# Retention and FFN of a hybrid decoder block: two state buffers, two results per PSUM bank, and another chunk order in the FFN

## The chip, the cores and the metric

The kernel runs on all 8 cores of one Trainium2 chip. Each core does one half (1024 own positions) of one of four sequences; cores exchange nothing. The metric is the device time in microseconds of the slowest core. An engine here is one of TensorE (PE, matmuls; PEld is its weight load), VectorE (DVE), ScalarE (ACT), GpSimd (POOL, which here only issues the weight loads) and SyncE (SP, which issues the other DMAs).

## What is computed

The block runs MoBA attention and RetNet retention side by side, merges them by sigmoid gates, and ends in a gated MLP with a causal depthwise convolution of width 3. Cut to the two parts that matter here:

```python
# retention, per head, chunks of 128 positions
scores = einsum('bhnid,bhnjd->bhnij', qc, kc) * inner_decay
inner  = einsum('bhnij,bhnje->bhnie', scores, vc)
kv     = einsum('bhnjd,bhnje->nbhde', kc * k_decay, vc)
def step(state, kv_n):                     # state is (128, 256) per head
    return chunk_decay * state + kv_n, state
_, prev = scan(step, 0, kv)
cross  = einsum('bhnid,nbhde->bhnie', qc * q_decay, prev)
yr     = head_group_norm(inner + cross, g) * silu(gr)
# FFN
u = causal_depthwise_conv(h2 @ w_up, conv_w, conv_b)
val, gt = split(u, 2)
x = x + gate2 * ((silu(gt) * val) @ w_down)
```

## The kernel before

The program lists its operations in one order in Python. A small scheduler (`Sched`) puts each into the queue of its engine, in that order, and makes it wait, by semaphores, for the last writer and the readers of what it touches. Each engine works its queue strictly in order. What counts as the same memory is coarse: blocks of 512 bytes in SBUF, and a whole bank in PSUM (`keys`, which returns one key for every tile whose name begins with `ps`). Two results in different halves of one bank are therefore one thing to the scheduler. `bank()` hands out the eight PSUM banks in rotation; weights come as slabs of 256 columns through `slab_load`, with four slab buffers in rotation, issued on POOL. `mm` is line 378, `tp` 382, `act` 399, `ts` 408 (one scalar) or 410 (two), `tt` 413, `stt` 419, `recip` 422, `acopy` 428, `vcopy` 431.

**Retention** (four groups `rg` of two heads `m`, eight heads in all). A group projects q and k with rotary. Then each head does, in this order:

1. `proj_tm` projects vr: 16 tiles of 128 positions, two to a bank, 256 matmuls of 256 columns, each bank evacuated by one VectorE cast.
2. The kv part: for n = 0 to 14 one matmul of `kdT` chunk n with `vr` chunk n into 256 columns of a bank of its own. VectorE copies the first into the state `Sst`, and updates the state in place with each further one (`stt`: state times decay plus product). At n = 7 ScalarE copies the state to `Sbh`; at n = 8 VectorE multiplies it by `flag` (`ts`); from n = 8 on ScalarE copies it to `Sb[n-8]` before VectorE may overwrite it; after the last update it is copied to `Sb[7]`.
3. Scores: eight matmuls of 128 columns, four to a bank; VectorE multiplies them by the decay into `sT`, and q by its decay into `qdT` (8 and 8 products).
4. The gate projection, 8 tiles, 128 matmuls of 256 columns in four banks. Each bank is copied by VectorE into `sgtmp` and put through a silu on ScalarE. A halo of two positions follows (16 matmuls, `psh`), copied into `ynh`.
5. Eight group norms c = 0 to 7: two matmuls (`sT`, `qdT`) into 256 columns of a bank of its own, then `groupnorm_gate`: bn_stats and bn_aggr on VectorE, a square root on ScalarE, and on VectorE the reciprocal, an affine that reads the bank (`ts`, L410), and two products. A small ninth for the halo, with `ynh` as its scratch tile, ends the head.

**FFN up part** (22 pairs `fp`). A pair has two slabs of `w_up`: `slv` for the value, `slg` for the gate. `up_chunk` does one chunk: two banks of 16 matmuls of 512 columns, a halo of 16 matmuls of 2 columns, and then on VectorE `conv`: two `ts` over 512 columns, four wide `stt` and four of one or two columns. For each of m = 0, 1 come value chunk, gate chunk, the silu of `ug` on ScalarE into `sgt`, and the product with `uv` on VectorE into `actT`. The buffers `uv`, `ug` and `sgt` alternate with the pair's m. At eight values of fp (1, 4, 7, 10, 13, 16, 19, 21) `mod_row_slab` comes first, 16 matmuls that read `s_rep2`. `s_rep2` lies right behind `sgt[1]` and shares its last 512-byte block.

Of the kernel before, what the change touches and what calls it, by code (L numbers as in the profile page):

```python
# [8 lines left out]
F32 = mybir.dt.float32  # L9
BF16 = mybir.dt.bfloat16  # L10
ALU = mybir.AluOpType
AF = mybir.ActivationFunctionType
# [256 lines left out]
def build_program(stop_after=None, debug=()):  # L269
# [10 lines left out]
    cd = _const_tables(1)["chunk_decay"]  # L280
    X1KEYS = [("x1s", d) for d in range(8)]

    with contextlib.ExitStack() as st:
# [38 lines left out]
        AA = Arena(A_t, 98304)  # L322
# [19 lines left out]
        flag = CA.alloc(F32, [128, 1])  # L342
# [34 lines left out]
        def mm(out, lhsT, rhs, start, stop):  # L377
            S.op("pe", lambda e: e.matmul(out, lhsT, rhs, start=start, stop=stop),  # L378
                 reads=[lhsT, rhs], writes=[out])
# [21 lines left out]
        def ts(out, in0, s1, s2, op0, op1=None):  # L401
            r = [in0]
            if not isinstance(s1, float):
                r.append(s1)
            if s2 is not None and not isinstance(s2, float):
                r.append(s2)
            if op1 is None:
                S.op("dve", lambda e: e.tensor_scalar(out, in0, s1, None, op0), reads=r, writes=[out])
            else:
                S.op("dve", lambda e: e.tensor_scalar(out, in0, s1, s2, op0, op1), reads=r, writes=[out])  # L410

        def tt(out, in0, in1, op):
            S.op("dve", lambda e: e.tensor_tensor(out, in0, in1, op), reads=[in0, in1], writes=[out])  # L413

        def stt(out, in0, sc, in1, op0, op1):
            r = [in0, in1]
            if not isinstance(sc, float):
                r.append(sc)
            S.op("dve", lambda e: e.scalar_tensor_tensor(out, in0, sc, in1, op0, op1), reads=r, writes=[out])  # L419
# [7 lines left out]
        def acopy(out, in_):  # L427
            S.op("act", lambda e: e.copy(out, in_), reads=[in_], writes=[out])

        def vcopy(out, in_):  # L430
            S.op("dve", lambda e: e.tensor_copy(out, in_), reads=[in_], writes=[out])  # L431
# [11 lines left out]
        def bank():  # L443
            b = bank_ctr[0] % 8
            bank_ctr[0] += 1
            return psb[b][:]
# [319 lines left out]
        Sb = AA.alloc(BF16, [128, 8, 256])  # L766
# [8 lines left out]
        Sbh = AA.alloc(BF16, [128, 256])  # L775
        zth = AA.alloc(BF16, [128, 512])
        ynh = AA.alloc(F32, [128, 256])
# [1 line left out]
        rgb = AA.alloc(F32, [128, 512])  # L779
        decTh = AA.alloc(F32, [128, 128])  # L780
        qdech = AA.alloc(F32, [128, 128])
        Sst = AA.alloc(F32, [128, 256])
        r32a = [AA.alloc(F32, [128, 512]) for _ in range(2)]
        r32b = [AA.alloc(F32, [128, 512]) for _ in range(2)]
        yn = [AA.alloc(F32, [128, 256]) for _ in range(2)]
# [22 lines left out]
        for rg in range(4):  # L808
# [20 lines left out]
            for m in range(2):  # L829
                h = 2 * rg + m  # L830
# [8 lines left out]
            for m in range(2):  # L839
                h = 2 * rg + m  # L840
# [2 lines left out]
                slv = slab_load(din["w_in"], 0, NKC, 5120 + h * 256)  # L843
                proj_tm(slv, list(range(16)), lambda i: vr[:, i:i + 2, :])
                for n in range(15):
                    o = bank()[:, 0:256]
                    mm(o, kdT[:, m, n, :], vr[:, n, :], True, True)
                    if n == 0:
                        vcopy(Sst, o)
                    else:  # L850
                        if n == 7:
                            acopy(Sbh, Sst)
                        if n == 8:
                            ts(Sst, Sst, flag[:, 0:1], None, ALU.mult)
                        if n >= 8:
                            acopy(Sb[:, n - 8, :], Sst)
                        stt(Sst, Sst, cd[h], o, ALU.mult, ALU.add)
                acopy(Sb[:, 7, :], Sst)
                for c4 in range(2):
                    pss = bank()  # L860
                    for u in range(4):
# [16 lines left out]
                vcopy(ynh[0:2, :], psh[0:2, 0:256])  # L878
                act(sgh[0:2, :], ynh[0:2, :], AF.Silu)
                for c in range(8):  # L880
                    o = bank()[:, 0:256]
                    mm(o, sT[:, c, :], vr[:, 8 + c, :], True, False)
                    mm(o, qdT[:, c, :], Sb[:, c, :], False, True)
                    groupnorm_gate(o, 128, c % 2, rgb[:, m * 256:(m + 1) * 256], sg[:, c, :], yn[c % 2],
                                   zt[:, c, m * 256:(m + 1) * 256])
# [174 lines left out]
        def up_chunk(sl, m, ch, dst, hi):  # L1060
            ps2 = [proj_fm(sl, m, lambda kc, th=th: h2T[:, kc, th * 512:(th + 1) * 512]) for th in range(2)]
            psh = proj_fm(sl, m, lambda kc: h2Th[:, kc, :], w=2)
            ts(Phs[:, hi, :], psh[:, 0:2], flag[:, 0:1], None, ALU.mult)
            conv(dst, ps2, Phs[:, hi, :], ch)

        fctr = [0]
        for fp in range(22):
            g2sched = {1: 0, 4: 1, 7: 2, 10: 3, 13: 4, 16: 5, 19: 6, 21: 7}
            if fp in g2sched:
                mod_row_slab(5, g2bc, s_rep2, g2sched[fp])  # L1070
            slv = slab_load(din["w_up"], 0, NKC, fp * 256)
            slg = slab_load(din["w_up"], 0, NKC, FFN + fp * 256)
            for m in range(2):
                fc = fp * 2 + m
                i = fctr[0] % 2
                fctr[0] += 1
                up_chunk(slv, m, fc, uv[i], 0)
                up_chunk(slg, m, 44 + fc, ug[i], 1)
                act(sgt[i], ug[i], AF.Silu)
                tt(actT[:, fc, :], uv[i], sgt[i], ALU.mult)  # L1080
        dump("actT", actT, [128, NFC, 1024], BF16)
        if stop_after == "H":
            return finish()
# [52 lines left out]
```

How the kernel before makes its waits and increments, by code:

```python
                def body(engobj):  # L117
                    waited = {}
                    for rec in ops[e]:
                        need = {}
                        for (de, di) in rec["deps"]:
                            drec = ops[de][di]
                            s = ("d", drec["dma"]) if drec["dma"] is not None else ("e", de)
                            need[s] = max(need.get(s, 0), drec["cnt"])
                        for s, v in need.items():
                            if waited.get(s, 0) >= v:
                                continue
                            waited[s] = v
                            sem = dsem[s[1]] if s[0] == "d" else esem[s[1]]
                            engobj.wait_ge(sem, v)
                        ins = rec["fn"](engobj)
                        if rec["dma"] is not None:
                            ins.then_inc(dsem[rec["dma"]], 16)
                        elif rec["signal"]:
                            ins.then_inc(esem[e], 1)
                    if e == "sp":
                        for k in final_wait:
                            engobj.wait_ge(dsem[k], 16 * self.dma_cnt[k])
```

## Time and profile before

| | us |
|---|---|
| median of 2 runs | 4114.99 (4110.7 and 4119.28) |
| profiled execution, device time | 4106.44 |
| its span on core 3, the slowest | 4104.8 (the cores: 4080.4 to 4104.8) |
| TensorE busy | 3050.6 (74%) |
| VectorE busy | 2048.4 (50%) |
| ScalarE busy | 496.5 (12%) |
| mean granted clock of TensorE, all cores | 0.843 to 0.846 |

All rows shown in this document are of the slowest core. In a timeline row the first number is the start in us from the span's beginning, the second how long the row lasts (x4 means four instructions merged), and the bracket gives the engine's idle time just before it with what ended it. A granted clock of 1.00 is 2.4 GHz on TensorE and 0.50 is 1.2 GHz. Matmul ends are modelled, so starts are surer than ends.

### The profile page before, as it was taken

The numbers are of one execution on the slowest core, as the hardware profiler recorded it, in microseconds if no ns is written. First come the engines' busy times: TensorE is split into PE (matmuls) and PEld (weight loads), VectorE is DVE, ScalarE is ACT, GpSimd is POOL, SyncE is SP. The second block draws the span as 40 slices with busy tenths as digits, with TensorE's granted clock in tenths as the row PEclk, the third lists the DMA queues.
The fourth block names the chain that finished last, engine by engine and source line by source line (L and its number), as shares of the span: only waits on it lengthen the run. The fifth ranks groups of instructions, "written<-read, shape, count | busy, mean of one in ns | idle before, by whom it ended". The sixth has DMA issues, their size and how long they took to land.

```text
span 4104.8 us, 57818 instructions; the slowest of 8 cores (4080.4 to 4104.8 us)
## 1 busy us (share of the span) xinstructions
PE 3050.6 (74%) x21160; PEld 1826.4 (44%) x21160; DVE 2048.4 (50%) x4111; ACT 496.5 (12%) x1016; POOL 218.3 (5%) x198
## 2 busy tenths in 40 slices
PE   0137767878678876766775999986368888888999
PEld 0122522325323553534554444455334444444888
DVE  0287555576555546455455322222377777776111
ACT  0021023311223010111111111100110000000000
POOL 1100000000000000000000010011000000000000
PEclk9998955589555888887887999987679999999999
DMA  9932200012000223123231866799935555555785
GB/s 117 152 118 31 27 5 1 3 34 32 11 1 1 51 28 66 23 57 42 44 53 17 130 83 84 90 158 179 176 64 73 72 72 73 72 72 80 119 139 96
DMA packets 435370, 282.02 MB, mean 69 GB/s; under 512 B 6794, under 2 KB 422794, under 8 KB 431506
## 3 DMA queue, kind: packets, MB, share of 16 engines
q0 software_dynamic: 384176, 195.10, 38.2%
q1 hardware_dynamic: 50916, 83.22, 6.8%
q8 instruction: 174, 2.85, 0.3%
q14 instruction: 104, 0.85, 0.1%
HBM read 452.41 MB, written 20.97 MB: 115 GB/s over the span
## 4 chain that ended last, share of the span: by engine, by line
PE 52%; DVE 27%; DMA 9%; issue 7%; ACT 4%; DVEq 1%; ACTq 0%; SPq 0%; POOL 0%; POOLq 0%
PE ps L378 50%; DVE hT L419 6%; DVE A L422 5%; DMA slab<-w_ada 5%; DVE hT L410 5%; DVE A L413 2%; ACT A L399 2%; DVE A L419 2%; DMA slab<-w_o 2%; PE ps L382 2%; DVE A L410 1%; DVE A L431 1%; ACT hT L399 1%; DVEq L130 1%; DVE C L799 1%
## 5 line engine op out<-in xcount | busy, mean ns | idle before, releaser
L378 PE MATMUL ps<-hT,slab 128*128 128x512 bf16 (+1 forms) x6144 | 1343.2, 377 | 2.8 <-DVE A L431 1.8
L378 PEld LDWEIGHTS ps<-hT,slab 128*128 128x128 bf16 x6144 | 584.6, 99 | 696.3 <-issue 56.5
L378 PE MATMUL ps<-slab,hT 128*128 128x256 bf16 (+1 forms) x4352 | 518.9, 285 | 101.5 <-ACT hT L399 93.0
L378 PE MATMUL ps<-A 128*128 128x256 bf16 (+3 forms) x1560 | 475.1, 363 | 115.7 <-ACT A L399 83.5
L378 PEld LDWEIGHTS ps<-slab,hT 128*128 128x128 bf16 (+1 forms) x4352 | 440.1, 102 | 177.8 <-issue 108.4
L399 ACT ACTIVATE A<-A 128x256 bf16<-128x256 f32 (+6 forms) x744 | 341.8, 470 | 1282.3 <-DVE A L431 596.9
L378 PE MATMUL ps<-slab,A 128*128 128x256 bf16 x3968 | 452.3, 278 | 46.5 <-DMA slab<-w_o 34.3
L378 PEld LDWEIGHTS ps<-slab,A 128*128 128x128 bf16 x3968 | 395.0, 100 | 99.9 <-issue 46.9
L378 PEld LDWEIGHTS ps<-A 128*128 128x128 bf16 (+1 forms) x1560 | 173.3, 113 | 411.5 <-issue 384.0
L419 DVE SCALAR_TENSOR_TENSOR hT<-ps,hT 128x511 f32<-128x511 f32 (+1 forms) x528 | 301.9, 572 | 56.1 <-DVE hT L419 1.4
L378 PE MATMUL ps<-A,C 128*128 128x256 bf16 (+3 forms) x552 | 210.3, 384 | 118.6 <-ACT A L399 98.1
L410 DVE TENSOR_SCALAR A<-ps,C 128x256 f32<-128x256 f32 (+2 forms) x432 | 196.6, 467 | 169.5 <-PE ps L378 93.2
L413 DVE TENSOR_TENSOR A<-ps,A 128x512 f32<-128x512 f32 (+5 forms) x360 | 181.3, 511 | 180.9 <-PE ps L378 123.3
L378 PE MATMUL ps<-C,slab 128*128 128x2 bf16 x3328 | 106.7, 164 | 206.2 <-DMA slab<-w_ada 131.2
L431 DVE COPY A<-ps 128x512 f32<-128x512 f32 (+2 forms) x216 | 117.5, 551 | 264.6 <-PE ps L378 217.2
L431 DVE CAST A<-ps 128x512 bf16<-128x512 f32 (+1 forms) x144 | 96.7, 686 | 265.3 <-PE ps L378 237.4
L378 PEld LDWEIGHTS ps<-C,slab 128*128 128x128 bf16 x3328 | 105.0, 97 | 237.9 <-issue 209.5
L413 DVE TENSOR_TENSOR ps<-ps,A 128x256 f32<-128x256 f32 x136 | 58.5, 430 | 271.7 <-PE ps L378 268.2
L422 DVE RECIPROCAL A<-A 128x512 f32<-128x512 f32 (+1 forms) x56 | 162.2, 2897 | 49.3 <-ACT A L399 49.3
L399 ACT ACTIVATE hT<-hT 128x1024 f32<-128x1024 f32 (+1 forms) x52 | 61.8, 1188 | 1015.3 <-DVE hT L419 646.7
L369 POOL DMA_DIRECT2D slab<-w_in x52 | 60.2, 1159 | 2095.4 <-PE ps L378 1506.4
L378 PE MATMUL ps<-C,A 128*128 128x2 bf16 (+1 forms) x136 | 12.8, 168 | 201.0 <-DVE C L800 174.7
(69 smaller groups left out, 1557.8 us busy)
## 6 DMA issues: line engine op xcount, KB each, us to landing
slab<-w_in POOLq DMA_DIRECT2D x52, 1024.0 KB, 9.2
slab<-w_ada POOLq DMA_DIRECT2D x48, 1024.0 KB, 22.5
slab<-w_up POOLq DMA_DIRECT2D x44, 1024.0 KB, 9.5
A<-xw SPq DMA_DIRECT2D x24, 1024.0 KB, 7.2
hT<-x1s SPq DMA_DIRECT2D x16, 1024.0 KB, 8.1
slab<-w_down POOLq DMA_DIRECT2D x16, 1024.0 KB, 9.7
slab<-w_ret_br POOLq DMA_DIRECT2D x8, 1024.0 KB, 10.6
slab<-w_o POOLq DMA_DIRECT2D x8, 1024.0 KB, 33.9
```

Of the source, the lines that this page charges most:

```text
L130: engobj.wait_ge(sem, v)
L369: S.op("pool", lambda e: e.dma_start(out=out, in_=in_), reads=reads, writes=writes, dma=key)
L378: S.op("pe", lambda e: e.matmul(out, lhsT, rhs, start=start, stop=stop), reads=[lhsT, rhs], writes=[out])
L382: S.op("pe", lambda e: e.matmul(out, in_, ident, start=True, stop=True), reads=[in_, ident], writes=[out])
L399: S.op("act", lambda e: e.activation(out, in_, func, **kw), reads=r, writes=w)
L410: S.op("dve", lambda e: e.tensor_scalar(out, in0, s1, s2, op0, op1), reads=r, writes=[out])
L413: S.op("dve", lambda e: e.tensor_tensor(out, in0, in1, op), reads=[in0, in1], writes=[out])
L419: S.op("dve", lambda e: e.scalar_tensor_tensor(out, in0, sc, in1, op0, op1), reads=r, writes=[out])
L422: S.op("dve", lambda e: e.reciprocal(out, in_), reads=[in_], writes=[out])
L431: S.op("dve", lambda e: e.tensor_copy(out, in_), reads=[in_], writes=[out])
L799: S.op("dve", lambda e: e.bn_stats(bnst[0:np_, bi, :], o), reads=[o], writes=[bnst[0:np_, bi, :]])
```

## The change

Four edits, in three places of the program.

```diff
-        Sst = AA.alloc(F32, [128, 256])
+        Sst2 = [AA.alloc(F32, [128, 256]), ynh]
...
                 for n in range(15):
-                    o = bank()[:, 0:256]
+                    if n % 2 == 0:
+                        pskv = bank()
+                    o = pskv[:, (n % 2) * 256:(n % 2) * 256 + 256]
                     mm(o, kdT[:, m, n, :], vr[:, n, :], True, True)
+                    cur, nxt = Sst2[n % 2], Sst2[(n + 1) % 2]
                     if n == 0:
-                        vcopy(Sst, o)
+                        vcopy(nxt, o)
                     else:
                         if n == 7:
-                            acopy(Sbh, Sst)
+                            acopy(Sbh, cur)
                         if n == 8:
-                            ts(Sst, Sst, flag[:, 0:1], None, ALU.mult)
+                            ts(cur, cur, flag[:, 0:1], None, ALU.mult)
                         if n >= 8:
-                            acopy(Sb[:, n - 8, :], Sst)
-                        stt(Sst, Sst, cd[h], o, ALU.mult, ALU.add)
-                acopy(Sb[:, 7, :], Sst)
+                            acopy(Sb[:, n - 8, :], cur)
+                        stt(nxt, cur, cd[h], o, ALU.mult, ALU.add)
+                acopy(Sb[:, 7, :], Sst2[1])
...
                 for c in range(8):
-                    o = bank()[:, 0:256]
+                    if c % 2 == 0:
+                        psy = bank()
+                    o = psy[:, (c % 2) * 256:(c % 2) * 256 + 256]
...
             for m in range(2):
+                up_chunk(slv, m, fp * 2 + m, uv[m], 0)
+            for m in range(2):
                 fc = fp * 2 + m
-                i = fctr[0] % 2
-                fctr[0] += 1
-                up_chunk(slv, m, fc, uv[i], 0)
-                up_chunk(slg, m, 44 + fc, ug[i], 1)
-                act(sgt[i], ug[i], AF.Silu)
-                tt(actT[:, fc, :], uv[i], sgt[i], ALU.mult)
+                up_chunk(slg, m, 44 + fc, ug[m], 1)
+                act(sgt[m], ug[m], AF.Silu)
+                tt(actT[:, fc, :], uv[m], sgt[m], ALU.mult)
```

The state alternates between a buffer of its own and the halo's scratch tile `ynh`: each update reads one and writes the other. Two kv products, and two group norms, share a bank, left half and right half. The FFN does both value chunks of a pair before its gate chunks. The number and kinds of instructions on every engine stay the same.

TensorE in the kv part of the first head, its end: products n = 11 to 14 (128x256 into a bank `psN`, `A<-` the arena that holds kdT and vr), the scores (128x128), and the first tile of the gate projection (from slab and hT; d_15 is its slab's DMA). Before:

```order
L378 MATMUL ps3<-A 128x256 [waits s_dve]
L378 MATMUL ps4<-A 128x256 [waits s_dve]
L378 MATMUL ps5<-A 128x256 [waits s_dve]
L378 MATMUL ps6<-A 128x256 [waits s_dve]
L378 MATMUL ps7<-A 128x128 [waits s_dve]
L378 MATMUL ps7<-A 128x128 x3
L378 MATMUL ps0<-A 128x128 [waits s_dve]
L378 MATMUL ps0<-A 128x128 x3
L378 MATMUL ps1<-slab,hT 128x256 [waits s_dve,d_15]
L378 MATMUL ps1<-slab,hT 128x256 x31
```

After the change the same place, from n = 10:

```order
L378 MATMUL ps5<-A 128x256
L378 MATMUL ps5<-A 128x256 [waits s_dve]
L378 MATMUL ps6<-A 128x256
L378 MATMUL ps6<-A 128x256 [waits s_dve]
L378 MATMUL ps7<-A 128x256
L378 MATMUL ps0<-A 128x128 x4
L378 MATMUL ps1<-A 128x128 x4
L378 MATMUL ps2<-slab,hT 128x256 [waits d_15]
L378 MATMUL ps2<-slab,hT 128x256 x31
```

Every product before waits for VectorE (s_dve) in a bank eight allocations old; after it, the left half (first of two rows with one bank) waits for nothing, the right half waits for VectorE to have read the left one, and scores and gate projection have no wait for VectorE.

TensorE in the group norms of the same head, two matmuls to a norm (the first of `sT`, the second of `qdT`), c = 1 to 3, before:

```order
L378 MATMUL ps7<-A 128x256
L378 MATMUL ps7<-A 128x256 [waits s_act]
L378 MATMUL ps0<-A 128x256
L378 MATMUL ps0<-A 128x256 [waits s_dve,s_act]
L378 MATMUL ps1<-A 128x256 [waits s_dve]
L378 MATMUL ps1<-A 128x256 [waits s_act]
```

After the change, the same three norms:

```order
L378 MATMUL ps7<-A 128x256 [waits s_dve]
L378 MATMUL ps7<-A 128x256 [waits s_act]
L378 MATMUL ps0<-A 128x256
L378 MATMUL ps0<-A 128x256 [waits s_act]
L378 MATMUL ps0<-A 128x256 [waits s_dve]
L378 MATMUL ps0<-A 128x256 [waits s_act]
```

c = 1 and c = 3 now share a bank with the norm ahead of them, and their first matmul waits for VectorE.

VectorE in the second pair of the FFN, where the second chunk's conv ends (banks 2, 3) and the third's begins (halo in ps7, banks 5, 6), before, where the second chunk is the gate chunk of m = 0:

```order
L419 SCALAR_TENSOR_TENSOR hT<-ps2,hT 128x1
L419 SCALAR_TENSOR_TENSOR hT<-ps2,hT 128x2
L419 SCALAR_TENSOR_TENSOR hT<-C,hT 128x1
L419 SCALAR_TENSOR_TENSOR hT<-C,hT 128x2
L413 TENSOR_TENSOR A<-hT 128x1024
L408 TENSOR_SCALAR C<-ps7,C 128x2
L410 TENSOR_SCALAR hT<-ps5,hT 128x512
L410 TENSOR_SCALAR hT<-ps6,hT 128x512
```

After the change, where the second chunk is the value chunk of m = 1 and the third is the gate chunk of m = 0:

```order
L419 SCALAR_TENSOR_TENSOR hT<-ps2,hT 128x1
L419 SCALAR_TENSOR_TENSOR hT<-ps2,hT 128x2
L419 SCALAR_TENSOR_TENSOR hT<-C,hT 128x1
L419 SCALAR_TENSOR_TENSOR hT<-C,hT 128x2
L408 TENSOR_SCALAR C<-ps7,C 128x2
L410 TENSOR_SCALAR hT<-ps5,hT 128x512
L410 TENSOR_SCALAR hT<-ps6,hT 128x512
```

The product (L413, 128x1024) is gone from between them; it now stands behind the third chunk, and the other behind the fourth as before.

## Rows read from the trace of the kernel before

**Rows 1.** windows: retention, FFN up part; stretch, busy per engine (instructions), PEclk, DMA, GB/s
```profile
1374.00:2310.00 936.00, 657.50 (x4906) 468.58 (x4903) 484.31 (x1119) 100.69 (x213) 31.42 (x28) 0.84 0.30 49
...
3014.00:3789.00 775.00, 675.65 (x4358) 331.01 (x4356) 548.38 (x1048) 46.72 (x44) 59.23 (x52) 0.93 0.55 70
```

**Rows 2.** timeline of one kv part; start, us, engine, line, operation [idle before <-releaser]
```profile
1659.13 0.41 DVE L431 COPY A<-ps 128x256 f32<-128x256 f32 x1
...
1659.65 0.42 DVE L419 SCALAR_TENSOR_TENSOR A<-A,ps 128x256 f32<-128x256 f32 x1
...
1660.22 0.27 PE L378 MATMUL ps<-A 128*128 128x256 bf16 x1 [0.26 <-DVE A L419]
...
1660.84 2.00 DVE L419 SCALAR_TENSOR_TENSOR A<-A,ps 128x256 f32<-128x256 f32 x4 [0.17 <-DVE A L419]
...
1664.09 0.35 DVE L408 TENSOR_SCALAR A<-A,C 128x256 f32<-128x256 f32 x1
...
1666.98 17.81 PE L378 MATMUL ps<-slab,hT 128*128 128x256 bf16 x144 [0.67 <-DVE A L419]
...
1672.25 0.42 DVE L419 SCALAR_TENSOR_TENSOR A<-A,ps 128x256 f32<-128x256 f32 x1 [0.72 <-ACT A L428]
1672.59 2.46 DVE L413 TENSOR_TENSOR A<-ps,A 128x128 bf16<-128x128 f32 x8
```

**Rows 3.** timeline, first and last of the eight heads: kv's first evacuation, gate projection
```profile
1431.46 0.41 DVE L431 COPY A<-ps 128x256 f32<-128x256 f32 x1
...
1439.17 17.39 PE L378 MATMUL ps<-slab,hT 128*128 128x256 bf16 x144 [0.57 <-DVE A L419]
...
2199.95 0.41 DVE L431 COPY A<-ps 128x256 f32<-128x256 f32 x1
...
2207.56 17.19 PE L378 MATMUL ps<-slab,hT 128*128 128x256 bf16 x144 [0.57 <-DVE A L419]
```

**Rows 4.** timeline of another head's kv part: one product at half clock
```profile
1746.21 0.37 PE L378 MATMUL ps<-A 128*128 128x256 bf16 x1 [0.26 <-DVE A L419]
1746.73 0.42 DVE L419 SCALAR_TENSOR_TENSOR A<-A,ps 128x256 f32<-128x256 f32 x1 [0.66 <-PE ps L378]
```

**Rows 5.** timeline of VectorE, group norms of one head: eight full ones, then the halo's
```profile
1691.33 0.54 DVE L410 TENSOR_SCALAR A<-ps,C 128x256 f32<-128x256 f32 x1
...
1692.85 0.42 DVE L799 BATCH_NORM_STATS2 C<-ps 128x6 f32<-128x256 f32 x1
...
1712.04 0.42 DVE L799 BATCH_NORM_STATS2 C<-ps 2x6 f32<-2x256 f32 x1 [0.84 <-PE ps L378]
```

**Rows 6.** waits (total us, times, longest) and lines by form, retention stage
```profile
DVE A L419 <- ACT A L428: 40.1, 57, 1.0
...
L431 DVE COPY A<-ps 2x256 f32<-2x256 f32 x8 | 3.3, 411 | 3.3 <-PE ps L378 3.3
```

**Rows 7.** windows around gate and vr projection; the column after POOL is the granted clock
```profile
1663.50:1666.90 3.40, 1.17 (x8) 0.70 (x8) 1.62 (x4) 0.84 (x3) 0.00 (x0) 0.57 1.39 187
1666.90:1670.00 3.10, 3.02 (x15) 2.19 (x16) 0.88 (x3) 1.18 (x3) 0.00 (x0) 0.50 0.05 7
...
1671.00:1672.00 1.00, 1.00 (x12) 0.89 (x10) 0.42 (x1) 0.33 (x1) 0.00 (x0) 1.00 0.00 0
...
1720.00:1741.00 21.00, 21.00 (x195) 18.81 (x194) 4.15 (x6) 0.00 (x0) 0.00 (x0) 1.00 0.00 1
```

**Rows 8.** timeline of VectorE after a drain in the FFN; last row from the waits
```profile
3172.17 0.22 DVE L408 TENSOR_SCALAR C<-ps,C 128x2 f32<-128x2 f32 x1 [8.15 <-PE ps L378]
...
3179.48 0.22 DVE L408 TENSOR_SCALAR C<-ps,C 128x2 f32<-128x2 f32 x1 [0.59 <-PE ps L378]
...
3187.15 1.22 DVE L413 TENSOR_TENSOR A<-hT 128x1024 bf16<-128x1024 f32 x1 [1.31 <-ACT hT L399]
...
3202.62 1.23 DVE L413 TENSOR_TENSOR A<-hT 128x1024 bf16<-128x1024 f32 x1 [1.36 <-ACT hT L399]
...
PE ps L378 <- ACT hT L399: 93.0, 8, 12.1
```

## The prediction

> **What bounds the kernel now.** I read the spans and clocks first: the profiled run is 4106.4 us, 8.6 us under the median 4115.0, so my sum is made against 4106.4 and 8.6 is added at the end. Then the stretches by stage [rows 1]. The change touches two: retention (936 us, TensorE busy 657) and the FFN's up part (775 us, TensorE busy 676, VectorE 548).
>
> Retention, for each of its 8 heads, is a chain of turns. TensorE projects vr (256 matmuls), computes 15 kv products and the scores, projects the gate (128 matmuls), then waits for eight group norms. The timeline of one kv part [rows 2] shows how it runs now: each product has a bank of its own, so TensorE is up to eight products ahead and only waits for VectorE to free the bank of eight allocations ago (the matmul at 1660.22). VectorE takes a state update in 0.42 us, started every 0.53 us ((2.00-0.42)/3). For the later updates it hands over to ScalarE, which copies the single state away, before it may overwrite it: 40.1 us of VectorE waits over the stage [rows 6]. TensorE does not care: it starts the gate projection at 1666.98, when update 9 frees a bank, while VectorE works on until 1672.67 (1672.25+0.42). From kv's first evacuation (1659.13) to the gate projection is 7.85 us here, 7.71 in the first head and 7.61 in the last of the eight [rows 3].
>
> Who decides the end of the gate projection? VectorE sits idle for TensorE before the copy that ends it (the halo's, 2x256): 3.3 us over 8 heads, 0.4 each [rows 6]. So TensorE's start time passes to the end with nearly no slack, and the 40.1 us of handovers lie beside TensorE's projection.
>
> In the FFN, TensorE gives a chunk (two 512-column products and a halo) every 7.31 us (VectorE's starts at 3172.17 and 3179.48 both wait for it [rows 8]). VectorE needs 6.4 to 6.7 us for its conv (3172.17 to 3179.48-0.59; 3179.48 to 3187.15-1.31), plus per pair of chunks a wait of 1.31 us for the silu and a product of 1.22. So VectorE is the slower of the two, 15.5 us a pair (3187.15 to 3202.62) against 14.6, except just after a drain. Eight times, 93.0 us in all, TensorE waits [rows 8] for the last silu, because s_rep2 begins in the 512-byte block that ends sgt[1].
>
> **The change part by part.**
>
> *kv, packed.* Dependencies go by whole bank, so product n (odd) must wait until VectorE has read product n-1. A step then has a length that alternates. Odd: VectorE's end to the matmul's start 0.15 (update 1 ends at 1659.65+0.42=1660.07, the matmul starts at 1660.22 [rows 2]), the matmul 0.27 at full clock or 0.37 at half clock [rows 2, 4], 0.10 to 0.15 to VectorE (1746.58 to 1746.73 [rows 4]), the update 0.42: 0.94 to 0.99 warm, 1.04 to 1.09 cold. Even: the matmul follows its twin at once, so the update comes 0.52 to 0.59 after the last one ends. Step 8 has the flag multiplication too: 0.35 [rows 2] plus an update and two gaps of 0.10, 0.97, up to 1.05.
>
> TensorE gets past product 13 only after update 12. From the end of the first evacuation that is six odd steps (three warm at 0.97, three cold at 1.07: 6.1), five even at 0.55 (2.75), step 8 (1.0): 9.9 us. Then 0.15, products 13 and 14, and eight score matmuls of 128 columns. At full clock 195 matmuls of 256 columns take 21.0 us, 0.108 each [rows 7]; the half clock adds 0.10 (0.37 against 0.27), so 0.21, and half of that for 128 columns. The granted clock is 0.57 from 1663.5 to 1666.9 and 0.50 after it [rows 7], so I take cold: 2x0.21+8x0.105=1.26. Gate projection at 9.9+0.15+1.26=11.3 us after the evacuation's end; now it is 7.85-0.41=7.4. **Later by 3.9 us a head.** Where VectorE, not TensorE, came last before (the 0.4 is a mean), a tenth or two are lost: 3.75x8 = **+30 us**. Bounds: all warm and shortest, 6x0.94+5x0.52+0.97+0.15+0.65=10.0, +2.6 a head, +21; all cold and longest, 6x1.09+5x0.59+1.05+0.15+1.26=12.0, +4.6, +37.
>
> *Two state buffers.* They take ScalarE's copies out of the chain: update n writes the other buffer, whose copy began two updates before. VectorE would have finished update 14 at 9.9+1.07+0.55=11.5 us instead of 13.1 (1672.67-1659.54 [rows 2]). Those 1.6 us are worth nothing: what comes next for VectorE (16 products, 2.46 us for 8 [rows 2], so until 16.4) is done before TensorE's second gate pair at 11.3+2x32x0.108=18.2, and each further one comes 3.5 us later. ynh as the second buffer adds only orders on VectorE that are met anyway.
>
> *Group norm, packed.* Product c (odd) now waits until VectorE's affine of c-1 has read the bank. Between that affine's end (1691.33+0.54) and the next bn_stats (1692.85) lie 0.98 us in which VectorE does its other two products [rows 5]. The round trip VectorE, two cold 256-column matmuls, VectorE is on record: 0.84 us idle at 1712.04 [rows 5]. It fits with 0.14 to spare: cost 0. Without that cover it would be 0.84 x 4 x 8 = 27 us; a shortfall of 0.1 gives 3.
>
> A rule speaks against packing. By these rows TensorE runs eight banks ahead in kv, and loses that lead. The Trainium skill, Perfetto Trace Analysis, section Matmul Optimizations, says "Ensure all 8 PSUM banks are being leveraged to maximize available instruction-level parallelism"; for kv the trace agrees (my 11.3 us against 7.4). Taken literally for the group norms too, the rule would charge the 27 us that the 0.98 us gap hides.
>
> *FFN order.* v0 g0 v1 g1 becomes v0 v1 g0 g1. TensorE's work and its rate stay. VectorE still has each product right behind its own silu, so the wait of 1.31 us [rows 8] stays, at all 44 products. What differs is the start after a drain. Now: v0, wait 0.59, g0, silu wait and product (1.31+1.22), by which time v1 has been there for a while. After: v0, wait 0.59, v1, then another wait for TensorE (3179.48+7.31=3186.79, a conv that starts at 3179.48 is done at 3185.84: 0.95). **0.9 us** later, not made good, since VectorE has no idle time until the next drain. Nine such stretches (the start and eight drains): **+8 us**; 0 to 8.5. slv's slots come free 7.3 us earlier, but no wait for a weight slab exists here to be shortened. The last chunk before each drain is g1 in both, so the 93.0 us stay.
>
> *Queues.* DMAs are neither added nor moved among themselves. 88 fewer banks are drawn over 8 heads, a multiple of 8, so later stages meet the same bank numbers.
>
> **Sum:** 4106.4+30+8 = 4144.4 in the profile's terms, with 8.6 beside the median **4153 us**, 0.9% slower.
>
> **The rivals.**
>
> *A, VectorE decides (not slower).* If the end of a head followed VectorE's chain and not TensorE's, the handovers removed would count: 1.6 us a head, 13 us less, and with +8 in the FFN 4101 (4110 beside the median). It decides if TensorE's gate projection has over 3.9 us of slack. Against it: VectorE is seen idle for TensorE right there [rows 6]. Chance 0.08.
>
> *B, the clock stays low (clearly slower).* TensorE idles longer in kv. Today the granted clock is 0.50 for the first 3 us of the gate projection and recovers by 1671 [rows 7]. If it stayed low through all 128 matmuls, the some 100 that now run at full clock cost 0.10 more each: 10 us a head, 80 in all: 4233, as much as 2%. Against: after the group norms TensorE has idled for 22 us and more, and by 1720, 9 us into the next projection, it has the full clock [rows 7]. A 4 us longer gap is mild. By the Trainium skill, TensorE: Matmul & The Clock Gate, section What's actually happening, idleness halves the clock and sustained work releases it; the trace agrees with its 0.50 and 1.00. Chance 0.03.
>
> *C, the group norms are exposed.* If the second matmul's result reached VectorE as late as if nothing hid it, +27 us: 4180 beside the median. For it: only 0.14 us is spare. Against: a small shortfall costs a tenth, not the whole. Chance 0.06.
>
> *Forecast as above.* 0.83.
>
> **How the numbers follow.** Lowest of the forecast: 4106.4+21+0=4127, highest 4106.4+37+8.5+3=4155; with 8.6, and 5 us for scatter (the two runs read 4110.7 and 4119.3), the likeliest case alone is 4131 to 4169. The range 4122 to 4174 takes in part of C's 4180 and leaves out A and B. A measurement here tells about 2% (82 us) from no change. Over 2% slower: B, and a little for what I have not seen, 0.04. Over 2% faster needs 82 us where the whole kv parts last 8x13: 0.01. Within 2%: 0.95.
>
> **What would show it.** In kv: update pairs every 1.5 to 1.65 us, alternating short and long gaps, TensorE's wait for VectorE in half the products, no wait of VectorE for ScalarE, and the first evacuation to the gate projection at 11 to 12 us; the copy 2x256 with a VectorE wait of several us. Group norms still 2.97 us apart. FFN: about 104 us between drains instead of 103. I am wrong if the first evacuation to the gate projection stays under 10 us, if that shift does not reach the head's end, or if the group norms' pace changes.

## The result, and the profile after

| | before | after |
|---|---|---|
| median of all runs, us | 4118.1 | 4211.7 |
| fastest run, us | 4101.0 | 4148.0 |
| ratio after to before | | 1.0123, 95% interval 1.0066 to 1.0181 |
| profiled execution, us | 4106.4 | 4163.9 |
| spans of the eight cores, us | 4080.4 to 4104.8 | 4120.2 to 4162.4 |

The changed kernel is 1.2% slower. The median of all its runs is no measure, since in about half of them the cores of one die had a lower clock and the time was up to 4476 us; the ratio leaves such runs of both kernels out. The forecast was 4153 us; 4118.1x1.0123 is 4169. The profiled execution lies some 14 us above the fastest ones: from the last head to the FFN, where the change touches nothing, its slowest core took 790 us, another core of the same execution 771, and the profiled core of before 762. On the slowest cores of the two kernels and of nine of the ten experiments (all but the first with the FFN order alone), this unchanged stretch takes 762 to 790 us, so a difference of under 28 us between two single device times says little. So I compare stretches, not whole spans. Rows of after are of its core 7, the slowest.

The first fence answers [rows 1]: windows of retention and of the FFN's up part after the change (same columns; the second is moved to where the FFN now lies).

```profile
1374.00:2310.00 936.00, 647.85 (x4732) 456.08 (x4730) 469.64 (x1092) 100.59 (x211) 28.26 (x25) 0.81 0.28 46
3065.00:3840.00 775.00, 677.64 (x4368) 331.58 (x4365) 541.46 (x1039) 46.57 (x44) 58.09 (x51) 0.93 0.54 70
```

By the first row, retention holds fewer matmuls in the same 936 us (4732 against 4906) at a lower granted clock (0.81 against 0.84). The FFN's shares are nearly those of before.

The next fence is the timeline of the first head's kv part after the change, and answers [rows 2] and [rows 4].

```profile
1422.99 0.41 DVE L431 COPY A<-ps 128x256 f32<-128x256 f32 x1
...
1423.55 0.38 PE L378 MATMUL ps<-A 128*128 128x256 bf16 x2 [1.17 <-DVE A L431]
1423.92 0.42 DVE L419 SCALAR_TENSOR_TENSOR A<-A,ps 128x256 f32<-128x256 f32 x1 [0.52 <-PE ps L378]
1424.52 0.42 DVE L419 SCALAR_TENSOR_TENSOR A<-A,ps 128x256 f32<-128x256 f32 x1 [0.17 <-DVE A L419]
...
1425.09 0.38 PE L378 MATMUL ps<-A 128*128 128x256 bf16 x2 [1.16 <-DVE A L419]
...
1430.33 0.58 PE L378 MATMUL ps<-A 128*128 128x256 bf16 x2 [1.51 <-DVE A L419]
1430.95 0.42 DVE L419 SCALAR_TENSOR_TENSOR A<-A,ps 128x256 f32<-128x256 f32 x1 [0.76 <-PE ps L378]
...
1435.12 17.37 PE L378 MATMUL ps<-slab,hT 128*128 128x256 bf16 x144
```

The matmul rows come as pairs now (x2: the right half of one bank and the left half of the next), each started 0.15 us after an update's end: 1424.52+0.42=1424.94, matmuls at 1425.09. The updates come in twos. The gate projection (x144) starts at 1435.12, 12.13 us after the first evacuation; in the last head it is 12.02:

```profile
2219.51 0.41 DVE L431 COPY A<-ps 128x256 f32<-128x256 f32 x1
...
2231.53 8.66 PE L378 MATMUL ps<-slab,hT 128*128 128x256 bf16 x70
```

Over the eight heads the mean of this distance is 12.24 us (11.85 to 12.66) against 7.76 before. It is nearly the whole of the story in retention: 4.5 of the 4.8 us by which a head grows. The next rows are the group norms of the first head and answer [rows 5]:

```profile
1455.68 0.54 DVE L410 TENSOR_SCALAR A<-ps,C 128x256 f32<-128x256 f32 x1
...
1456.37 1.01 PE L378 MATMUL ps<-A 128*128 128x256 bf16 x4 [3.55 <-DVE A L410]
...
1457.27 0.42 DVE L799 BATCH_NORM_STATS2 C<-ps 128x6 f32<-128x256 f32 x1
...
1461.73 0.55 DVE L410 TENSOR_SCALAR A<-ps,C 128x256 f32<-128x256 f32 x1
...
1462.42 1.01 PE L378 MATMUL ps<-A 128*128 128x256 bf16 x4 [5.05 <-DVE A L410]
1463.26 0.42 DVE L799 BATCH_NORM_STATS2 C<-ps 128x6 f32<-128x256 f32 x1
```

Norm 1's matmuls (x4 with norm 2's) start 0.15 us after the affine's end (1456.22), and bn_stats comes at 1457.27, 1.05 us after that end; norm 3's comes at 1463.26, 0.98 after 1462.28. Both are as before the change, where norm 1 of the first head had the same 1.05 us (1459.74+0.54 to 1461.33) with a bank of its own:

```profile
1459.74 0.54 DVE L410 TENSOR_SCALAR A<-ps,C 128x256 f32<-128x256 f32 x1
...
1461.33 0.42 DVE L799 BATCH_NORM_STATS2 C<-ps 128x6 f32<-128x256 f32 x1
```

Waits over the stage (total us, times, longest) and a line by form, both after the change, answer [rows 6]:

```profile
PE ps L378 <- DVE A L410: 149.5, 32, 5.4
...
DVE A L419 <- ACT A L428: 7.3, 11, 0.7
```

```profile
L431 DVE COPY A<-ps 2x256 f32<-2x256 f32 x8 | 3.3, 412 | 8.5 <-PE ps L378 8.5
```

TensorE waits 149.5 us for the affines, in 32 places, and VectorE's pace in the norms does not change. VectorE's waits for ScalarE's state copies fell from 40.1 us to 7.3. The forecast was none, and the rows behind the 7.3 need not be real waits: update 11 of the first head starts at 1432.73, just after a copy that ended at 1432.58, but the copy that it depends on by the program had ended at 1431.86. VectorE's wait before the halo's copy rose from 3.3 to 8.5 us, 1.0 to 1.15 us in every head: TensorE is now plainly the last to come. The clock answers [rows 7]:

```profile
1427.00:1435.00 8.00, 2.87 (x16) 1.43 (x16) 4.19 (x11) 2.96 (x8) 0.00 (x0) 0.55 0.66 90
1435.00:1438.00 3.00, 3.00 (x18) 2.14 (x16) 2.54 (x10) 0.69 (x2) 0.00 (x0) 0.51 0.03 8
1438.00:1440.00 2.00, 2.00 (x20) 1.80 (x19) 1.62 (x7) 0.00 (x0) 0.00 (x0) 1.00 0.00 0
```

After the gate projection's start the clock stays at half for nearly three microseconds more. The FFN answers [rows 8], the timeline of VectorE after a drain, then a row of the waits:

```profile
3120.29 0.22 DVE L408 TENSOR_SCALAR C<-ps,C 128x2 f32<-128x2 f32 x1 [8.12 <-PE ps L378]
...
3127.70 0.22 DVE L408 TENSOR_SCALAR C<-ps,C 128x2 f32<-128x2 f32 x1 [1.03 <-PE ps L378]
...
3134.91 0.22 DVE L408 TENSOR_SCALAR C<-ps,C 128x2 f32<-128x2 f32 x1 [0.49 <-PE ps L378]
...
3142.58 1.23 DVE L413 TENSOR_TENSOR A<-hT 128x1024 bf16<-128x1024 f32 x1 [1.31 <-ACT hT L399]
```

```profile
PE ps L378 <- ACT hT L399: 97.1, 8, 13.1
```

VectorE waits 1.03 us for TensorE before the second chunk and 0.49 before the third. The wait before the third is new; the two together are 1.52 us, where the forecast had 0.59 and 0.95. The product of m = 0 begins at 3142.58, 22.29 us after the start of the first conv, with three convs ahead of it; it was 14.98 before, with two.

### The profile page after: what moved, and what is told of

Its sections match the earlier page's. It is cut to its first block, busy times and chain, and to the rows that moved or that the text cites. A ratio compares the mean times of both kernels' runs of the same rounds, so it can differ in the third digit from the quotient of the medians.

```text
span 4162.4 us, 57672 instructions; the slowest of 8 cores (4120.2 to 4162.4 us)
## 1 busy us (share of the span) xinstructions
PE 3067.4 (74%) x21160; PEld 1826.8 (44%) x21160; DVE 2048.8 (49%) x4111; ACT 497.1 (12%) x1016; POOL 218.2 (5%) x198
## 4 chain that ended last, share of the span: by engine, by line
PE 58%; DVE 23%; DMA 9%; issue 6%; ACT 3%; DVEq 1%; ACTq 0%; SPq 0%; POOL 0%; POOLq 0%
PE ps L378 56%; DVE A L422 5%; DVE hT L410 4%; DMA slab<-w_ada 3%; DVE hT L419 3%; DVE A L413 2%; DVE A L419 2%; DMA A<-xw 2%; ACT A L399 2%; PE ps L382 2%; DVE A L410 1%; DVE A L431 1%; DMA slab<-w_o 1%; DVEq L130 1%; DVE C L799 1%
## 5 line engine op out<-in xcount | busy, mean ns | idle before, releaser
L378 PE MATMUL ps<-A 128*128 128x256 bf16 (+3 forms) x1560 | 492.6, 377 | 305.9 <-DVE A L410 149.5
L413 DVE TENSOR_TENSOR A<-ps,A 128x512 f32<-128x512 f32 (+5 forms) x360 | 181.3, 511 | 172.3 <-PE ps L378 117.3
L413 DVE TENSOR_TENSOR ps<-ps,A 128x256 f32<-128x256 f32 x136 | 58.5, 430 | 293.7 <-PE ps L378 290.2
L413 DVE TENSOR_TENSOR A<-A 128x512 bf16<-128x512 f32 (+5 forms) x289 | 135.2, 475 | 33.3 <-DMA A<-b_g 5.6
```

## The experiments

In the numbers below, "gate" is the mean distance over eight heads from kv's first evacuation to the start of the gate projection, "head" the mean from that evacuation to the halo's bn_stats, and "FFN" the stretch from the first 512-column matmul to the first down matmul. "Device" is the time of the profiled execution in us, or, as a number near 1, the ratio to the kernel before, which was run beside each.

| kernel | gate | head | FFN | device |
|---|---|---|---|---|
| before | 7.76 | 52.2 | 775.0 | 4106, medians 4118 to 4122 |
| after | 12.24 | 57.0 | 781.5 | 1.0123 |
| kv unpacked | 6.43 | 51.6 | 781.1 | 0.9993 |
| buffers only | 6.44 | 51.7 | 774.7 | 4105 |
| norms only | 7.75 | 52.1 | 776.4 | 4103 |
| FFN order only | 7.9 | 52.6 | 783.3 | 4119 |
| kv packed only | 13.82 | 58.7 | 779.1 | 4160 |
| kv in pairs | 3.37 | 48.0 | 781.1 | 4115 |
| FFN aligned | 7.9 | 52.9 | 664.0 | 4006 |
| after, FFN aligned | 12.28 | 57.0 | 666.0 | 4050 |
| all that helped | 3.45 | 47.9 | 665.1 | 0.9624 |

**One edit undone: kv unpacked.** The kernel after, with

```diff
-                    if n % 2 == 0:
-                        pskv = bank()
-                    o = pskv[:, (n % 2) * 256:(n % 2) * 256 + 256]
+                    o = bank()[:, 0:256]
                     mm(o, kdT[:, m, n, :], vr[:, n, :], True, True)
```

> The changed kernel with one edit undone: each kv product has a bank of its own again; the two state buffers, the packed group norms and the new FFN order stay. My theory: the loss sits in TensorE's wait inside the kv part. The gate projection then starts when update 9 frees its bank, and with two buffers update 9 ends at about 7 x 0.55 + 1.0 + 0.55 = 5.4 us after the first evacuation's end, so first evacuation to gate projection is about 6.1 us (7.8 before, 12.2 changed). The head (first evacuation to the halo's bn_stats) is about 50.6 us (52.2 before, 57.0 changed), the FFN stretch stays at 782. Device time about 6 us under the kernel before. Rival (the buffers or the packed norms cost, not the kv packing): first evacuation to gate projection stays near 12, device time stays 40 to 50 us above the kernel before.

Gate 6.43 us (expected 6.1), head 51.6 us, FFN 781.1 us, ratio 0.9993 (0.9979 to 1.0008). The whole loss of the change goes with this edit (what is left of it, 6 us more in the FFN and 5 us less in the eight heads, cancels). In the timeline of its first head (VectorE, then TensorE):

```profile
1424.11 0.41 DVE L431 COPY A<-ps 128x256 f32<-128x256 f32 x1
...
1425.29 0.42 DVE L419 SCALAR_TENSOR_TENSOR A<-A,ps 128x256 f32<-128x256 f32 x1 [0.17 <-DVE A L419]
...
1425.89 0.42 DVE L419 SCALAR_TENSOR_TENSOR A<-A,ps 128x256 f32<-128x256 f32 x1 [0.17 <-DVE A L419]
...
1430.40 17.84 PE L378 MATMUL ps<-slab,hT 128*128 128x256 bf16 x144
```

the updates follow each other every 0.59 us with no alternation, and the gate projection starts 6.29 us after the evacuation. The head is 51.6, not the 50.6 I expected: the next experiment says why.

**The two buffers alone.** The kernel before with `Sst2`, `cur` and `nxt` as in the diff of the change, and nothing else.

> The kernel before with the two state buffers alone. Theory that TensorE's place in the order decides: VectorE's chain to update 9 is shorter by the handovers, so the gate projection starts 1.6 us earlier (6.1 us after the first evacuation against 7.8), the head takes 50.6 us against 52.2, 13 us less over eight heads. Theory that VectorE's chain decides: update 14 ends 4 to 5 us earlier and the head gets shorter by that, 48 us, 35 us less in all. Theory that the buffers are worth nothing because the copies lie beside TensorE's projection: 52.2.

Gate 6.44 us (expected 6.1), 1.3 us earlier than before; head 51.7 us, so only 0.5 us of it arrived (4 us over eight heads), and the stretch from the gate projection's start to the first bn_stats is 18.57 us where it was 17.80. VectorE's chain does not decide, or the gain would be 4 us a head. Windows after the start of the gate projection show where it went. The second head with the buffers alone (its gate projection starts at 1514.77):

```profile
1514.80:1518.00 3.20, 3.20 (x16) 2.21 (x17) 2.20 (x6) 2.03 (x6) 0.00 (x0) 0.50 0.63 85
1518.00:1520.00 2.00, 2.00 (x15) 1.52 (x14) 1.67 (x7) 0.27 (x1) 0.00 (x0) 0.70 0.00 0
```

The second head of the kernel before (start 1521.73):

```profile
1521.70:1524.00 2.30, 2.27 (x11) 1.61 (x12) 0.84 (x2) 0.90 (x3) 0.00 (x0) 0.50 0.03 4
1524.00:1526.00 2.00, 2.00 (x21) 1.76 (x19) 0.84 (x2) 0.64 (x2) 0.00 (x0) 1.00 0.00 0
```

With the buffers the clock is at half for 3.2 us and at 0.70 in the 2 us after; before it is at half for 2.3 us and at full speed in the next 2. The start of the dense work came earlier and the clock did not come with it.

The same can be counted in every head, with windows of 0.25 us over the first 7 us of the gate projection. The time at half clock in them is 2.8 us before (2.2 to 3.8), 4.4 us with the buffers alone (3.7 to 5.3) and 4.2 us with kv unpacked (3.8 to 5.2). In all 72 heads of the nine kernels without pairs, the stretch from the gate projection's start to the first bn_stats is 16.3 to 16.4 us plus half of that time. So the 1.6 us more at half clock are the missing 0.8 us, and TensorE decides when the norms start in every one of these heads.

How large this is depends on what it is held against. Four kernels have the kv part of before (before, norms only, FFN order only, FFN aligned), with heads of 52.2, 52.1, 52.6 and 52.9 us; in 5 of their 32 heads TensorE was at half clock for 5.2 to 5.9 us, in the other 27 for 2.2 to 3.8. Against their mean, 52.5 us, the two kernels with a gate of 6.4 gain 0.85 us a head out of 1.4.

**The packed group norms alone.** The kernel before with `psy` as in the diff.

> The kernel before with the packed group norms alone. My theory: the round trip of 0.84 us hides in the 0.98 us of the two products, so the norms stay 2.97 us apart and the stretch from the first bn_stats to the halo's stays at 26.6 us. Rival (exposed): four norms of eight start up to 0.8 us later, 29 to 30 us for the stretch, up to 27 us in all.

From the first bn_stats to the halo's, 26.6 us in the mean as before; head 52.1 us. VectorE's affines and bn_stats of the first head, from the affine of norm 0 on:

```profile
1443.38 0.55 DVE L410 TENSOR_SCALAR A<-ps,C 128x256 f32<-128x256 f32 x1
...
1444.96 0.42 DVE L799 BATCH_NORM_STATS2 C<-ps 128x6 f32<-128x256 f32 x1
...
1449.42 0.54 DVE L410 TENSOR_SCALAR A<-ps,C 128x256 f32<-128x256 f32 x1
...
1450.94 0.42 DVE L799 BATCH_NORM_STATS2 C<-ps 128x6 f32<-128x256 f32 x1
```

Norm 1 comes 1.03 us after the affine's end (1443.93 to 1444.96) and norm 3 0.98 after (1449.96 to 1450.94), as in the kernel before (1.05 and 0.98): hidden, as forecast, and these rows show no cost.

**The FFN order alone**, in two experiments with the same kernel.

> The kernel before with the new FFN order alone. My theory: VectorE waits for TensorE once more after each of the nine restarts, so the FFN stretch (first 512-column matmul to the first down matmul) is 782 us against 775, and retention heads stay at 52.2 us. Rival (the order changes nothing and the 7 us come from elsewhere): 775.

> The kernel before with the new FFN order alone, timed in rounds. My theory: 7 us more in the FFN stretch (782 against 775), heads at 52.2 us, so device time 4122 to 4125, a ratio of 1.001 to 1.003, which the interval may not clear. Rival (more than half of the 1.2% loss comes from the FFN): ratio 1.006 or more.

FFN 781.7 us in the first (read on core 7, whose span was 4104.9 us; the three device times were 4376 to 4426) and 783.3 us in the second. Over all kernels that share the old buffer layout, the stretch is 774.7 to 779.1 us with the old order (four kernels) and 781.1 to 783.3 with the new one (five). The means are 776.3 and 781.7, so the order costs 5 to 7 us, by stretches (after against before: 6.5). The whole time can't say it: the four device times of the second lie between 4118.8 and 4338.8, those of before beside them between 4113.8 and 4460.0, and there is no ratio. Against the rival, which wants 25 us, the stretch is far too small.

**kv packed, one buffer.**

> The kernel before with the kv products packed two to a bank, but still one state buffer. My theory: TensorE now follows VectorE's chain, so here ScalarE's handovers come onto TensorE's path: odd steps before 7 cost 1.0, even ones 0.55, each step from 7 on at least the 1.14 us of the single buffer, so update 12 ends 11.9 us after the first evacuation's end and the gate projection starts 13.7 us after the evacuation's start (7.8 before, 12.2 changed with two buffers). Head about 58.5 us, 50 us more than before in all. Rival (the second buffer is worth nothing under packing too): 12.2 and 57.0.

Gate 13.82 us against the 13.7 of my sum, head 58.7 us, device 4159.7. The same stretch of its timeline, steps 9 and 10:

```profile
1434.21 0.59 PE L378 MATMUL ps<-A 128*128 128x256 bf16 x2 [2.15 <-DVE A L419]
1434.80 0.42 DVE L419 SCALAR_TENSOR_TENSOR A<-A,ps 128x256 f32<-128x256 f32 x1 [0.73 <-PE ps L378]
...
1435.95 0.42 DVE L419 SCALAR_TENSOR_TENSOR A<-A,ps 128x256 f32<-128x256 f32 x1 [0.73 <-ACT A L428]
...
1436.52 0.58 PE L378 MATMUL ps<-A 128*128 128x256 bf16 x2 [1.72 <-DVE A L419]
```

Both updates wait 0.73 us, the first for TensorE and the second for ScalarE, and TensorE's next pair (1436.52) waits for them. Here the second buffer is worth 1.6 us a head (13.82 to 12.24), 13 us in all. Alone it brought the gate projection forward by 1.3: it is worth something where TensorE's next step waits for an update that stood behind ScalarE's copies.

**The same packing, another order: kv in pairs.** The kernel after, with both products of a bank issued before either is read:

```diff
                     if n % 2 == 0:
                         pskv = bank()
+                        for j in range(n, min(n + 2, 15)):
+                            mm(pskv[:, (j % 2) * 256:(j % 2) * 256 + 256], kdT[:, m, j, :], vr[:, j, :], True, True)
                     o = pskv[:, (n % 2) * 256:(n % 2) * 256 + 256]
-                    mm(o, kdT[:, m, n, :], vr[:, n, :], True, True)
```

> The changed kernel with one difference: both products of a bank are issued before VectorE reads either. Same packing, same buffers, same number of banks. My theory: the loss is the wait that the order within a bank makes, not the sharing. TensorE then never waits for VectorE inside kv; the gate's first bank was read by update 5, so the gate projection starts about 3.5 us after the first evacuation. The gate projection ends about 4 us earlier than before, unless VectorE's own work (updates until 8.7 us, 5 us of products, four copies at 1.65 us with a table load) comes last: head 48.5 to 50.5 us, against 57.0 changed and 52.2 before; device time 6 to 20 us under the kernel before. Rival (two results in a bank are slow in any order): first evacuation to gate projection stays above 11 us.

Its second head:

```profile
1503.04 1.80 PE L378 MATMUL ps<-A 128*128 128x256 bf16 x15
...
1503.91 0.41 DVE L431 COPY A<-ps 128x256 f32<-128x256 f32 x1
...
1507.17 15.97 PE L378 MATMUL ps<-slab,hT 128*128 128x256 bf16 x144 [0.74 <-DVE A L419]
```

All 15 products run in one row without a wait, and end (1504.84) about half a microsecond after VectorE's first copy does (1504.32). The gate projection starts 3.26 us after the evacuation (3.37 in the mean). Head 48.0 us: 9 us less than after the change and 4.3 less than before, a little below the 48.5 to 50.5 expected. So sharing a bank costs nothing that shows here; reading the left half between the two writes does. Its one device time, 4114.9, tells little: its cores took 4056 to 4113 us, on cores 0 to 3 4056 to 4086 and on cores 4 to 7 4068 to 4113. The 6 to 20 us under the kernel before that I expected can't be read from it (before beside it: 4116.5 and up).

Two things are new in these heads. In four of the eight the clock stays full over the first 7 us of the gate projection; in the other four it is at half for 3.4 us of them. And in the four at full clock the first bn_stats comes 17.3 to 18.0 us after that start, not 16.4: there TensorE no longer comes last. The likely last ones are VectorE and ScalarE with the copies and silus of the gate, as the expectation allowed for; no run separates them. In the second head VectorE waits 2.29 and 1.02 us for ScalarE among its last gate copies.

**The FFN's drains.** The kernel before, with one line ahead of `uv`:

```diff
+        HA.off = 1536
         uv = [HA.alloc(F32, [128, 1024]) for _ in range(2)]
```

> The kernel before, with the FFN's uv, ug, sgt and s_rep2 moved by 64 bytes so that none shares a 512-byte block with another. Theory: the 93 us that TensorE waits for the last silu at eight places come from that shared block alone. TensorE then runs into the next pair at once, VectorE is never drained, and the FFN stretch is VectorE's own work: 44 x 15.5 + 8 x 0.5 + 10 = 695 us against 775. Rival (a real dependency or the bank rotation makes the wait): 775, with the waits in the same places.

FFN 664.0 us against 775.0, device 4006.5: 111 us in the stretch, where I expected 80. The two rows of TensorE are the starts of two `mod_row_slab` in its timeline, the two of VectorE a conv's beginning:

```profile
3145.43 1.91 PE L378 MATMUL ps<-slab,hT 128*128 128x256 bf16 x16
...
3234.88 1.91 PE L378 MATMUL ps<-slab,hT 128*128 128x256 bf16 x16
...
3176.97 1.52 DVE L410 TENSOR_SCALAR hT<-ps,hT 128x512 f32<-128x512 f32 x2
3178.40 3.75 DVE L419 SCALAR_TENSOR_TENSOR hT<-ps,hT 128x511 f32<-128x511 f32 x6
```

From one to the next is 89.45 us, 12 chunks of 7.31 and the 16 matmuls (1.7 to 1.9), and neither row has an idle time in front. And VectorE is no longer the slower one, which is what my 695 had missed. The two wide `ts` take 1.52 us together where they took 1.72, the `stt` rows 3.75 where they took 3.95, and a conv is done 5.77 us after its start (3176.83 to 3182.60) where it took 6.36. In the list of its instructions two waits of VectorE for itself are gone from each conv (before the second `ts` and before the third wide `stt`), and the first wide `stt` now waits for the first `ts` instead of the second, because the halves of a 1024-wide tile no longer share a 512-byte block. Each of these three starts comes 0.2 us earlier: the second `ts` within its row, the first `stt` at 3178.40, 0.09 us before the `ts` row ends at 3178.49 (before the change it began 0.10 us after), and the third `stt` within its row. A pair then costs VectorE 14.0 us (products start at 3169.13 and 3183.91, with 0.79 of waiting for TensorE between them), and TensorE's 14.6 decides. The address moved by 64 bytes too, but the instructions themselves are as long as before: a 128x512 `ts` takes 803 ns in the mean (806 before), a 128x511 `stt` 741 (749) and a 128x510 one 749 (748). The gain lies between them.

**The changed kernel with the same line.**

> The changed kernel with the FFN's buffers moved by 64 bytes, so that no drain happens. Theory (the new FFN order costs one extra wait after each restart): without drains there are no restarts but the first, so the order costs at most 0.9 us: FFN stretch 664 to 666 us, as with the old order and the same move (664.0). Rival (the order costs in every pair): 670 us or more. Heads stay at 57.0 us; device time about 4040.

FFN 666.0 us, and between two `mod_row_slab` the same 89.44 us:

```profile
3187.39 1.91 PE L378 MATMUL ps<-slab,hT 128*128 128x256 bf16 x16
...
3276.83 1.91 PE L378 MATMUL ps<-slab,hT 128*128 128x256 bf16 x16
```

The new order costs nothing in the steady state. Of the 1.9 us against the old order, 1.2 lie ahead of the first `mod_row_slab`, where the first 32 matmuls took 9.76 us here and 8.58 there, and 0.7 behind the last one, in TensorE's wait for the last product before the down projection (6.02 us against 5.28). So the 5 to 7 us of the order come from the restarts, as forecast. The device time expected was 4040; the profiled execution took 4050, and the two others 4123 and 4185.

**A version that beats both kernels.** Before, with two buffers, kv in pairs, the aligned FFN, and each FFN product moved behind the next value chunk's conv:

```diff
                 up_chunk(slv, m, fc, uv[i], 0)
+                if pend_tt:
+                    pfc, pi = pend_tt.pop()
+                    tt(actT[:, pfc, :], uv[pi], sgt[pi], ALU.mult)
                 up_chunk(slg, m, 44 + fc, ug[i], 1)
                 act(sgt[i], ug[i], AF.Silu)
-                tt(actT[:, fc, :], uv[i], sgt[i], ALU.mult)
+                pend_tt.append((fc, i))
```

> The kernel before with two state buffers, kv products issued in pairs into shared banks, the aligned FFN buffers, and each FFN product moved behind the next value chunk's conv, so that the silu runs beside it. Theory: FFN stretch bound by TensorE at 44 x 14.62 + 8 x 3.5 = 671 us, or by VectorE at 44 x 14.2 = 625, whichever is more, so 671 to 680 against 775, and heads at 48.5 to 50.5 us against 52.2. Device time 105 to 130 us under the kernel before, ratio 0.968 to 0.975. Rival (slabs from HBM or the clock take the gain): FFN over 700 us with waits for slab DMAs, ratio above 0.98.

Ratio 0.9624 (0.9603 to 0.9645), median 3964.7 against 4121.9. The gain is larger than the 0.968 to 0.975 expected: the FFN took 665.1 us where 671 was the least expected, and a head 47.9 where 48.5 was. Against before they give 110 and 34 us; the some 10 us left are within the spread of the unchanged stretches. The waits of the FFN stretch in this kernel:

```profile
DVE C L408 <- PE ps L378: 88.3, 81, 2.8
...
PE ps L378 <- DVE hT L419: 5.2, 1, 5.2
DVE A L413 <- ACT hT L399: 1.3, 1, 1.3
```

VectorE's wait for the silu is gone (1.3 us once, where each of the 44 products waited some 1.3), and it bought nothing: 665.1 us against 664.0 with the alignment alone, since TensorE had already become the bound.

## Why the prediction was right

**TensorE's lead in kv decides: right, and sized too small.** The sum said the gate projection would start 3.9 us later; it starts 4.5 us later (12.24 against 7.76). In the first head the pairs of steps took 1.54, 1.54 and 1.60 us (said: 1.52), steps 7 and 8 2.10 (said: 2.07), and steps 9 to 12 1.85 and 1.71 (said: 1.62 each). The last two hold most of the missing part. I had taken 0.15 us from a half-clock matmul's end to VectorE, from one row; update 9 starts 0.62 us after its matmul (1430.33 to 1430.95) where 0.52 was taken. The rest is the same kind of small delay, and which of several waits ends it I can't separate.

**"A tenth or two are lost": wrong in sign.** I let 3.75 of 3.9 arrive. In fact all of it does, and the stretch from the gate projection's start to the norms lengthens from 17.80 to 18.02. The clock makes this 0.2: TensorE is at half clock for 3.25 us after that start where it was 2.84, and half of the difference is lost. It is no more than what the kernels with an unchanged kv part differ by (17.70 to 18.33). Together the head went from 52.21 to 56.97 us, +4.76, 38 us in all where I said 30 with bounds of 21 and 37. Against the mean of the four kernels with the old kv part, 52.5 us, it is 36 us, so whether the upper bound was passed can't be told; the 30 was too low by 6 to 8 us either way.

**Two buffers worth nothing: right beside the old kv, and I missed the other half.** I had them at nothing because VectorE comes last nowhere. But they also bring update 9 forward, and with it TensorE: 1.3 us earlier with banks of their own, of which the clock eats 0.5 to 0.8. Under packing they save 1.6 us a head, so my sum's 9.9 us already contained their worth without saying so.

**Norms hidden: right.** 26.72 us against 26.66 from first bn_stats to the halo's, and 26.65 with the norms alone, where rival C fell.

**FFN order: right.** Said +8 from nine restarts of 0.9; seven intervals between drains grew from 693.3 to 699.1 us in all, 0.83 each, and the stretch by 6.5.

**Signs that missed.** The first evacuation to the gate projection was to be 11 to 12 us and is 12.24; the pairs of updates 1.5 to 1.65 us, and the late ones take 1.7 to 1.85; the halo's copy was to wait several us, and waits 1.1. This last was read wrongly: VectorE already waits for TensorE at the gate copies just ahead of it, so the halo's copy can show only the last 1.0 to 1.15 us of a delay, and does so in the kernels with a gate of 6.4 too.

**The rivals.** A fell: the gate's delay reaches the head's end in full, and VectorE's copy waits longer than before. B fell: TensorE is at half clock for 1.7 to 4.8 us after the gate projection's start, by heads, and never through all of it. The eight heads (+38) and the FFN (+6.5) add to 45 us, 1.1%, inside the measured interval. Not all 38 show in the stretch from the first head's start to the last one's end, which grew by 32.2: between the fourth and fifth heads, where the change touches nothing, the profiled core of before took 97.2 us and that of after 90.9.

**The rule on PSUM banks**, from the Trainium skill (Perfetto Trace Analysis, Matmul Optimizations, "Ensure all 8 PSUM banks are being leveraged"), pointed the right way for kv here, but the kernel in pairs uses the same eight banks as the changed one and is 9 us a head faster. What counted was how many products TensorE could have issued before its first wait: 8 before, 1 after, 15 in pairs.

## What to carry to other kernels

When two results share a bank, write both before anything reads either; in the order write, read, write, the second write hangs on the reader, and everything queued behind it on TensorE hangs too. Shortening a chain on VectorE pays only in so far as TensorE waits for it, and TensorE's place in its queue after the wait decides what the chain is worth. Look at what the dependency tracker calls one thing: 64 bytes of padding were worth 111 us here, far more than all four edits.

## What I had not expected of the hardware

A start of dense matmuls moved earlier by 1.3 us kept TensorE at half clock for longer (4.4 us instead of 2.8 in the mean of eight heads), and 0.8 of the 1.3 us was lost. A start moved earlier by 4.4 us, behind shorter pauses of TensorE (0.16, 0.67 and 0.74 us in the second head's kv part, where before it was busy for 3.6 of 8 us), kept the full clock in four heads of eight. Waits of VectorE for its own last instruction, which looked free, were not: with two of them gone and a third moved one instruction back, a conv of eleven instructions took 5.77 us instead of 6.36, though each instruction took as long as before.
